# Two matmuls of 256 moving columns in the place of each one of 512, in the dense products of a two-block transformer kernel

## What is computed

```python
z = jnp.einsum("bsd,de->bse", h, w_in[i])            # (512 x 1024) . (1024 x 3488)
ya = jnp.einsum("bse,ed->bsd", oa, w_oa[i])
yb = jnp.einsum("bse,ed->bsd", ob, w_ob[i])
x = x + jnp.einsum("bsd,de->bse", merged, w_o[i])
u = jax.nn.relu(jnp.einsum("bsd,df->bsf", h2, w_up[i]))     # 1024 -> 4096
x = x + jnp.einsum("bsf,fd->bsd", u * u, w_down[i])         # 4096 -> 1024
gate = jax.nn.sigmoid(jnp.einsum("bsd,de->bse", h3, w_ple_gate[i]))
...
proj = h @ w_in                                             # gated DeltaNet
gu = h @ w_in                                               # SwiGLU, both layers
return (jax.nn.silu(gu[..., :D_FF_2]) * gu[..., D_FF_2:]) @ w_out
```

## Time and profile before

| | |
|---|---|
| time, median of 3 runs | 2178.96 us (2178.59 to 2181.84) |
| the profiled execution | 2178.25 us, of which the span is 2176.4 us |
| PE busy | 2128.5 us, 98% of the span |
| weight loads (PEld) busy | 1699.4 us, 78% |
| DVE, ACT busy | 1147.3 us, 814.4 us |
| granted TensorE clock, mean | 0.992 of full speed |

### The profile page before, as it was taken

How to read it: one execution, slowest core, us unless ns; L and a number is a source line. 1 busy time by engine, 2 the same in 40 slices (tenths; PEclk the granted TensorE clock), 3 DMA queues, 4 the chain that set the end, 5 groups by cost and what they waited for, 6 DMA issues and landing times.

```text
span 2176.4 us, 26174 instructions
## 1 busy us (share of the span) xinstructions
PE 2128.5 (98%) x10774; PEld 1699.4 (78%) x10774; DVE 1147.3 (53%) x1710; ACT 814.4 (37%) x1167; POOL 36.8 (2%) x40
## 2 busy tenths in 40 slices
PE   8999999999999999999999999999999999999998
PEld 6777678888888887787977888887787777888886
DVE  5575765442542578888836444423733746444323
ACT  4324753331232364542534222212414843332212
POOL 0120000000000000000100000000000000000000
PEclk9999999999999999999999999999999999999999
DMA  4221013222222213343121222223233022222221
GB/s 173 87 78 39 2 59 107 97 93 99 80 97 97 97 64 100 114 126 96 41 97 58 97 97 97 94 84 112 67 115 129 2 97 78 93 82 97 97 97 68
DMA packets 43112, 190.69 MB, mean 88 GB/s; under 512 B 15520, under 2 KB 16224, under 8 KB 22384
## 3 DMA queue, kind: packets, MB, share of 16 engines
q1 hardware_dynamic: 40656, 184.78, 25.3%
q10 hardware_dynamic: 2336, 4.23, 0.6%
HBM read 185.25 MB, written 3.74 MB: 87 GB/s over the span
## 4 chain that ended last, share of the span: by engine, by line
PE 51%; DVE 1%; ACT 1%; issue 0%; DVEq 0%; ACTq 0%
PE psum L441 14%; PE psum L440 14%; PE psum L442 14%; PE psum L898 1%; PE psum L881 1%; PE psum L911 1%; PE psum L451 1%; PE psum L455 1%; PE psum L452 1%; PE psum L2701 0%; PE psum L2767 0%; ACT weights_high L223 0%; DVE weights_low L250 0%; PE psum L2793 0%; PE psum L2754 0%
## 5 line engine op out<-in xcount | busy, mean ns | idle before, releaser
L250 DVE TENSOR_TENSOR weights_low<-weights_raw,weights_high 128x2048 fp32r<-128x2048 f32 (+1 forms) x161 | 365.5, 2270 | 587.9 <-ACT weights_high L223 587.8
L440 PE MATMUL psum<-split,weights_high 128*128 128x512 f32 x1448 | 574.5, 397 | 6.0 <-DVE weights_low L250 3.7
L441 PE MATMUL psum<-split,weights_high 128*128 128x512 f32 x1448 | 573.4, 396 | 0.0
L442 PE MATMUL psum<-split,weights_low 128*128 128x512 f32 x1448 | 571.8, 395 | 0.0
L223 ACT CAST weights_high<-weights_raw 128x2048 fp32r<-128x2048 f32 (+1 forms) x161 | 304.0, 1888 | 572.5 <-PE psum L442 532.9
L440 PEld LDWEIGHTS psum<-split,weights_high 128*128 128x128 f32 x1448 | 271.5, 188 | 76.7 <-issue 5.2
L442 PEld LDWEIGHTS psum<-split,weights_low 128*128 128x128 f32 x1448 | 271.5, 187 | 65.3
L441 PEld LDWEIGHTS psum<-split,weights_high 128*128 128x128 f32 x1448 | 271.6, 188 | 64.5 <-issue 0.2
L441 PE MATMUL psum<-hidden_low,weights_high 128*128 128x512 f32 x256 | 102.1, 399 | 0.0
L440 PE MATMUL psum<-hidden_high,weights_high 128*128 128x512 f32 x256 | 100.9, 394 | 0.0
L442 PE MATMUL psum<-hidden_high,weights_low 128*128 128x512 f32 x256 | 100.4, 392 | 0.0
(11 more groups left out here) (484 smaller groups left out, 3073.5 us busy)
## 6 DMA issues: line engine op xcount, KB each, us to landing
weights_raw<-in_weights SPq DMA_DIRECT2D x161, 1024.0 KB, 4.9
minus_c<-minus_c_rows ACTq DMA_DIRECT2D x16, 256.0 KB, 7.5
x_stream<-in_x SPq DMA_DIRECT2D x4, 512.0 KB, 7.2
gdn_in_grown<-gdn_rows SPq DMA_DIRECT2D x4, 512.0 KB, 4.5
chain_grown<-gdn_rows SPq DMA_DIRECT2D x4, 512.0 KB, 3.5
out<-end_results SPq DMA_DIRECT2D x8, 256.0 KB, 2.1
table<-rope_tables SPq DMA_DIRECT2D x1, 1024.0 KB, 12.4
weights_raw<-in_weights SPq DMA_DIRECT2D x1, 768.0 KB, 4.2
```

The costliest lines, as they stand in the source:

```text
L250: self.nc.vector.tensor_tensor(out=self.low_of(n)[:, 0:width], in0=self.raw[:, n % 2, 0:width], in1=self.high_of(n)[:, 0:width].bitcast(se ...
L440: nc.tensor.matmul(bank, wh, ah, start=first, stop=False)
L441: nc.tensor.matmul(bank, wh, al, start=False, stop=False)
L442: return nc.tensor.matmul(bank, wl, ah, start=False, stop=last)
```

## The change

`product` now cuts a moving tile of 512 columns into two halves of 256. It does the three matmuls on the first half of the bank and then the three on the second half, for each of the tiles over k. The stationary tiles are the same for both halves. A moving tile of another width would stay whole; there is none in the calls of `product`. The line numbers of what follows in the file rise by 4, and 440, 441, 442 become 443, 444, 445.

```diff
             (wh, wl), (ah, al) = w_parts, a_parts
-            nc.tensor.matmul(bank, wh, ah, start=first, stop=False)
-            nc.tensor.matmul(bank, wh, al, start=False, stop=False)
-            return nc.tensor.matmul(bank, wl, ah, start=False, stop=last)
+            width = ah.shape[-1]
+            halves = (slice(0, width // 2), slice(width // 2, width)) if width == T else (slice(0, width),)
+            for n, half in enumerate(halves):
+                nc.tensor.matmul(bank[:, half], wh, ah[:, half], start=first and n == 0, stop=False)
+                nc.tensor.matmul(bank[:, half], wh, al[:, half], start=False, stop=False)
+                done = nc.tensor.matmul(bank[:, half], wl, ah[:, half], start=False, stop=last and n == len(halves) - 1)
+            return done
```

## The result

| | before | changed |
|---|---|---|
| median | 2180.40 us (2178.59 to 2184.36, 4 runs) | 2221.98 us (2220.15 to 2222.68, 4 runs) |
| ratio, 95% interval | | 1.019 (1.0178 to 1.0202) |
| the profiled execution, its span | 2178.25 us, 2176.4 us | 2221.36 us, 2219.6 us |

The change costs 1.9%. Between the two profiled executions it is 43.1 us, where the sum had 28.7.

What follows compares the result with a forecast made beforehand. The prediction took PE's single stream of matmuls to bound the kernel. A switch of 2.8 ns and a load of 1.1 ns, times 7356, add 28.7 us to 2178.25: 2207 us, own range 2190 to 2235, 8-in-10 range 2174 to 2330.

Steps and rivals of the forecast that it cites:

- the sum: Whole kernel: 3.9 ns more for each of 7356 old matmuls, 28.7 us added; chance 0.47.
- PE's stream bounds the kernel, and the added price comes out 7356 times: Whole kernel: one stream of matmuls on PE, so any added cost per matmul of `product` shows 7356 times.
- One more matmul and one more load for each: In `product`: same columns pass, but each old matmul gains one matmul and one weight load, even with repeated weights.
- The load floor is 110 ns and lies below a half: In `product`: load plus matmul cost at least 110 ns, just under half of 233.1 (116.6), so loads stay hidden.
- The excess of 17 ns is paid by the column: In float32r matmuls of 512 columns: 233.1 ns exceeds estimates by 17 ns, taken as column price, not per matmul.
- Switch 2.8 ns, load 1.1 ns: Per old matmul in `product`: an extra switch, from float32 rows, and an extra load, from 16-column rows; 3.9 ns together.
- A fixed price for each shape: In `product`: one pace per shape, 233.1 ns for 512 columns and 118.5 for a half; 16 stationary columns about 1 ns sooner.
- the fixed cost: Rival for all float32r matmuls: each half pays 19.8 ns, 126.5 ns a half, 145.6 us added, 2324 us; chance 0.28.
- nothing at all: Rival for `product`: moving operand's supply alone sets the pace, two halves take 233 ns, 2178 us; chance 0.08.
- the faster case: Rival for `product`: the excess builds late in long streams, halves reach the load floor, 94.9 us gained, 2083 us; chance 0.09.
- the float32 rate: Rival for `product`: 256 columns too few for float32r's fast mode, 216.1 ns a half, 3643 us; chance 0.05.
- The bounds of the text on the pace: Sign in the MLP: the prediction is wrong if a half's pace is not between 117.5 and 121 ns.

Runs made afterwards that it cites:

- run 3: Changed kernel with the matmuls reordered so that two in a row use the same stationary tile; 2221.23 us, ratio 1.0194 over the kernel before.
- runs 1: Against the changed kernel: only MLP tiles cut, in turn 512, 384+128, 320+192, 256+256, four times 128, others whole; one execution, 2264.09 us.
- run 8: Only MLP tiles cut, in turn 448+64, 288+224, 272+240, 256+256, 176+168+168, where the changed kernel has halves everywhere; one execution, 2241.63 us.
- run 9: Changed kernel with every 512-column tile cut at column 272 instead of 256; 2212.66 us, ratio 1.0151 over the kernel before.
- run 2: Changed kernel with MLP up-projection stationary tiles narrowed to 128, 112, 96, 64 or 32 columns, moving tiles halved or whole; one execution, 2219.02 us.

## Why the prediction came out as it did

The forecast was slower by 28.7 us, by an added price of 3.9 ns for each old matmul; it was 43.1 us. The mechanism held, and one term of the sum was too small: the load's.

- *PE's stream bounds the kernel, and the added price comes out 7356 times.* Shown: PE's busy time grew by 44.7 us, where the span grew by 43.2, waits stayed within 1 us, and with a fifth of the matmuls cut 12 of the 42 us appeared.
- *One more matmul and one more load for each.* Shown by the records, 7356 more of both, and by run 3: the load is paid even for weights that are there.
- *The load floor is 110 ns and lies below a half.* Shown in runs 1 and 8: 111.7 ns at 128 columns and 335.0 / 3 = 111.7 at 176 and 168.
- *The excess of 17 ns is paid by the column.* This was the largest doubt, and it went the forecast's way. From 288 columns (244.2 - 111.7 = 132.5 ns, with the partner of 224 columns taken at the load floor) to 512 (233.3) it is 100.8 / 224 = 0.450 ns for each column, where the sum used 0.449; a price of 0.4166 with 19.8 ns for each matmul would have given 139.8 ns at 288 columns and is excluded. What is left without columns is 233.3 - 512 x 0.450 = 2.9 ns, with an uncertainty of 1 or 2.
- *Switch 2.8 ns, load 1.1 ns.* Their sum of 3.9 came out near for the cut at 272 (3.4 ns in run 8, 4.5 in run 9) and for the products with stationary activations (3.1 ns). It failed for the two equal halves with stationary weights, which are seven eighths of all: 6.7 ns. The load is the term that was mis-sized. With 16 stationary columns, where the load is short, two halves cost about 2 ns more than a whole matmul (234.2 to 232), close to the switch alone; with full loads 6.7, so some 4.7 ns go with the second full load, where the sum had 1.1. Between the two it does not rise evenly: by run 2 two halves cost 1.7 ns more than a whole with 32 stationary columns, 5.4 with 64 and 4.5 with 96. The prediction took the 1.1 ns of the 16-column rows, measured under a long stream, as the price of any load; its own range allowed for several times that, up to 7.7 ns in all. And even as a reading that 1.1 ns was weak, since whole matmuls with 32 stationary columns took 233.3 ns, as with 128.
- *A fixed price for each shape.* The prediction took one for granted, and no run bears it out. It is not the number of matmuls alone, since run 9 has the same number and pays less; not the load's length alone, since 112 stationary columns cost 120.0 ns in one chunk and 117.3 in another; and not the place of the operands alone. That counts, since 32 bytes took the halves from 120.0 to 118.7 ns, but in both pairs, the two chunks with 112 columns and the cut at 272 in runs 8 and 9, the operands lie alike and the pace differs.

The rivals: the fixed cost asked for 126.5 ns a half, nothing at all for 116.6, the faster case for 110 and the float32 rate for 216. Measured were 120.0, to which the 118.5 of the forecast lies nearest. The bounds of the text on the pace, 117.5 to 121 ns, held. That the pace fell inside those bounds owes something to luck: the load term was a quarter of the 4.7 ns, and came from ten steps of an uneven stream.

The Trainium skill, "TensorE: Matmul & The Clock Gate", section "LDWEIGHTS (loading the stationary operand)", gives P / 1.2 ns for a load of P columns, an estimate of 106.7 ns for 128. The measured floor for a load with its matmul is 111.7 ns, 5 more. The Trainium skill's warm gap of N / 2.4 + 2.5 ns, on the same page in "Back-to-back issue gap", has a fixed part near the 2.9 found here, but a column at 0.417 ns where float32r columns took 0.450.

What stays open is what sets the 1 to 3 ns: in part the places of the moving and the stationary tile, in part something that differs between two stretches with the same places, such as the rhythm into which the uneven steps fall. Three placements and two cuts don't give a rule, and the one rule that I tried, a line of 64 bytes more or less, is a supposition that predicted 43 us where 9 came.

## What to carry to other kernels

In a kernel that is one gapless stream of matmuls, price a change to their shape by the pace from start to start, and draw the law from several lengths: here some 3 ns for each matmul and 0.45 ns for each float32r column, and never less than the 112 ns of a full weight load. So with full weight loads whole tiles of 512 columns are the cheapest, the products in halves cost 1.3 to 2.9% more, anything under about 240 columns is paid as 240, and it doesn't help to repeat the same weights. Don't trust a difference of 1 or 2 ns that one short stretch shows: the same matmul kept two paces in two stretches. When such a stream fills the kernel, try the operands' start addresses too: 32 bytes of padding, with whole matmuls, made this kernel 0.4% faster than before (2172.11 us), which is the best version found.

## What was not expected of the hardware

- The same matmul shape has several paces, depending on the place of its operands: with 512 columns 233.3 ns for activations 32 bytes off a multiple of 64, and 232.4 on it, with the weights on one in both. With the weights 32 bytes off and the activations on it, the time was that of the kernel before (1.0003).
- The same places don't guarantee the same pace: with 112 stationary columns a half took 120.0 ns in one chunk and 117.3 in another of the same kernel that reads the same places, and 272 and 240 columns took 236.7 to 236.9 ns in run 8 and 237.8 in run 9.
- A whole float32r matmul with a full load has a faster pace than the 233.3 ns of most of the kernel: nine steps with the weights in `early_high` took 226.7 ns each.
- A stationary tile of 32 columns with 512 moving ones took 233.3 ns, no less than a full one, where 64 and 96 took 231.3 and 231.1.
- Uneven cuts can be cheaper than even ones: 272 and 240 columns took 236.7 ns in run 8 where 256 and 256 took 240.0, and in the whole kernel the cut at 272 saved 9 us over the cut at 256.
- Short float32r matmuls showed no slow mode: 128, 168 and 176 columns all ran at the load's pace of 111.7 ns, where the float32 price of a column would have given 143 ns and more for the latter two.
